# Modulation sums from GpSimd to VectorE, and column sums by transposes between feed-forward steps, in a two-part transformer kernel

## The reference

```
# first block, per layer (the mixer is "even" in layer 0, "odd" in layer 1)
h = h + 0.5 * rmsnorm(swiglu(rmsnorm(h, nw[0]), ...), nw[1])     # D_FF = 2816
h = h + rmsnorm(mixer(rmsnorm(h, nw[2])), nw[3])
h = h + 0.5 * rmsnorm(swiglu(rmsnorm(h, nw[4]), ...), nw[5])

# second block, per layer i
mod_l = silu(c) @ ada_w[i] + ada_b[i]          # (1024) @ (1024, 6144)
mod_c = silu(c_ctx) @ ada_w[i] + ada_b[i]      # only its first 2048 values, and only in layer 0, are used
sh1, sc1, g1, sh2, sc2, g2 = split(mod_l, 6)
h = rms_norm(x, norm1_g[i]) * (1 + sc1) + sh1
x = x + g1 * (diff_attention(h, h_c) if i == 0 else fourier_mix(h))
h2 = rms_norm(x, norm2_g[i]) * (1 + sc2) + sh2
x = x + g2 * (swiglu_2(h2) if i == 0 else moe_swiglu(h2))        # D_FF_2 = 3584, 8 experts
out = rms_norm(x, final_g)
```

## Time and profile before

| | |
|---|---|
| runs | 2940.45, 2946.97, 2948.32 us; median 2946.97 |
| profiled execution | span 2946.9 us from the first to the last instruction; its time is not given apart from the span |
| TensorE | 2758.8 us busy, 94%; mean granted clock 0.963 |
| VectorE | 2085.5 us busy, 71% |
| ScalarE | 1680.7 us busy, 57% |
| GpSimd | 590.6 us busy, 20% |
| DMA | 664.55 MB, mean 226 GB/s |
| chain that ended last | TensorE 81%, VectorE 12%, ScalarE 4%, issue 2% |

### The profile page before, as it was taken

The page is one execution under the profiler, slowest core; times in us unless marked ns, Lnnn a source line. Parts: engine busy times, 40 slices in busy tenths (PEclk is TensorE's granted clock), DMA queues, the critical chain, the costliest instruction groups (busy, mean ns, idle before and its releaser), DMA issues.

```text
span 2946.9 us, 35814 instructions
## 1 busy us (share of the span) xinstructions
PE 2758.8 (94%) x12921; PEld 2256.2 (77%) x12921; DVE 2085.5 (71%) x2339; ACT 1680.7 (57%) x2177; POOL 590.6 (20%) x321
## 2 busy tenths in 40 slices
PE   7999899989999999979669998799999999999997
PEld 6888778878987778868448886687878778787885
DVE  4556757678457755552557874699988989998897
ACT  4456454454367764432444442277787877778775
POOL 2000029999100000013009993000000000000000
PEclk9999999999899999989779999799999999999999
DMA  8555137678443345532028882299999999999994
GB/s 285 187 163 181 36 136 243 229 264 285 144 147 118 115 165 188 185 106 79 0 85 282 289 285 97 78 346 329 351 350 341 350 335 353 339 351 340 346 355 163
DMA packets 278012, 664.55 MB, mean 226 GB/s; under 512 B 12868, under 2 KB 21344, under 8 KB 277904
## 3 DMA queue, kind: packets, MB, share of 16 engines
q1 hardware_dynamic: 263344, 609.74, 58.4%
q0 software_dynamic: 14560, 53.36, 5.5%
HBM read 662.00 MB, written 1.05 MB: 225 GB/s over the span
## 4 chain that ended last, share of the span: by engine, by line
PE 81%; DVE 12%; ACT 4%; issue 2%; DMA 0%; DVEq 0%; ACTq 0%; SPq 0%
PE ps L2206 24%; PE ps L2208 24%; PE ps L2207 24%; DVE w_lo L1398 4%; ACT w_hi L742 2%; PE ps L2322 1%; PE ps L2388 1%; PE ps L2892 1%; PE ps L2806 1%; DVE xt L2078 1%; DVE small L1964 1%; PE ps L2768 1%; PE ps L2596 0%; DVE xn L1477 0%; PE ps L2850 0%
## 5 line engine op out<-in xcount | busy, mean ns | idle before, releaser
L1398 DVE TENSOR_TENSOR w_lo<-w_raw,w_hi 128x1024 fp32r<-128x1024 f32 x1156 | 1520.1, 1339 | 496.6 <-ACT w_hi L742 470.9
L742 ACT ACTIVATE w_hi<-w_raw 128x1024 fp32r<-128x1024 f32 x1156 | 1210.9, 1058 | 844.2 <-PE ps L2208 843.3
L2206 PE MATMUL ps<-w_hi,act_hi 128*128 128x512 f32 (+1 forms) x3424 | 1351.1, 395 | 50.7 <-DVE w_lo L1398 33.2
L2208 PE MATMUL ps<-w_lo,act_hi 128*128 128x512 f32 (+1 forms) x3424 | 1326.7, 387 | 0.0
L2207 PE MATMUL ps<-w_hi,act_lo 128*128 128x512 f32 (+1 forms) x3424 | 1325.6, 387 | 0.0
L2206 PEld LDWEIGHTS ps<-w_hi,act_hi 128*128 128x128 f32 x3424 | 650.2, 190 | 198.8 <-DVE w_lo L1398 53.9
L2208 PEld LDWEIGHTS ps<-w_lo,act_hi 128*128 128x128 f32 x3424 | 649.5, 190 | 132.6
L2207 PEld LDWEIGHTS ps<-w_hi,act_lo 128*128 128x128 f32 x3424 | 651.1, 190 | 126.0 <-issue 2.9
L621 POOL TENSOR_TENSOR scr<-scr 128x1024 f32<-128x1024 f32 x98 | 285.5, 2913 | 8.2
L619 POOL TENSOR_SCALAR scr<-scr,small 128x1024 f32<-128x1024 f32 x98 | 189.5, 1934 | 6.4
L602 POOL DMA_DIRECT2D scr<-in_ada_w x48 | 36.8, 766 | 401.7 <-DVE h L1482 382.3
(11 more groups left out here) (454 smaller groups left out, 1682.0 us busy)
## 6 DMA issues: line engine op xcount, KB each, us to landing
w_raw<-in_moe_w SPq DMA_DIRECT2D x336, 1024.0 KB, 6.8
scr<-in_ada_w POOLq DMA_DIRECT2D x48, 1024.0 KB, 5.9
w_raw<-in_ffn_w_gate SPq DMA_DIRECT2D x44, 1024.0 KB, 5.3
w_raw<-in_ffn_w_up SPq DMA_DIRECT2D x44, 1024.0 KB, 5.3
w_raw<-in_ffn_w_down SPq DMA_DIRECT2D x44, 1024.0 KB, 4.9
w_raw<-in_ff_w SPq DMA_DIRECT2D x42, 1024.0 KB, 5.7
w_raw<-in_odd_w_in SPq DMA_DIRECT2D x20, 1024.0 KB, 5.1
w_raw<-in_even_w_in SPq DMA_DIRECT2D x14, 1024.0 KB, 5.2
```

The source lines that it names most:

```text
L742: act.activation(w_hi[:, g % SPLITS, 0:c * width], w_raw[:, s % RING, o:o + c * width], ACT.Copy).then_inc(hi_done, 1)
L1398: dve.tensor_tensor(w_lo[:, g % SPLITS, 0:c * width], w_raw[:, s % RING, o:o + c * width], w_hi[:, g % SPLITS, 0:c * width].bitcast(F32), ...
L2206: pe.matmul(out_ap, hi, whi, start=start, stop=False)
L2208: return pe.matmul(out_ap, hi, wlo, start=False, stop=stop)
```

## The change

GpSimd keeps only the loads of the weight chunks, each released by a count of sums (`ada_sum`). The sums are done by VectorE as one instruction each, dst = w * x + dst (`accumulate`): 64 for layer 0, 48 for layer 1. They are strewn between the `w_lo` of the second and third feed-forward (layer 0, 0.625 for each granule) and of the dense one (layer 1, 0.6875 for each granule); a credit counter decides behind which.

The sum over partitions is now: TensorE transposes a block of 128x1024 sums in eight 128x128 transposes into banks 4 and 5 (`turn_sums`), once silu has read these; VectorE adds up each 128 columns of the result (`column_sums`) into `m_cols`. There are eight such windows for layer 0 (`SUMS_FIRST`, `SUMS_SECOND`: two in the second feed-forward, one in every step of the third) and six for layer 1 (`SUMS_DENSE`: steps 1 to 6). TensorE's gate matmuls of the next step wait for the adds (`mod_red`). The small instructions that make `modv` and `modc` follow once per layer.

```diff
 def modulation(l):          # GpSimd
     load(0)
     load(1)
     for j in range(24):
-        nb, k = divmod(j, 4)
-        cols = slice(DM * nb, DM * (nb + 1))
-        pool.wait_ge(ada_in[j % 2], n(ada_in[j % 2], 16))
-        for c in range(2):
-            sums = [(m_sumc, 8)] if l == 0 and nb < 2 else []
-            for dst, of in sums + [(m_sum, 0)]:
...
-                pool.tensor_scalar(product, w, x, 0.0, ALU.mult, ALU.add).then_inc(ada_mul, 1)
-                pool.wait_ge(ada_mul, n(ada_mul))
-                pool.tensor_tensor(dst[:, cols], dst[:, cols], product, ALU.add).then_inc(ada_sum, 1)
-            pool.wait_ge(ada_sum, n(ada_sum, 1 + len(sums)))
+        n(ada_sum, 4 if l == 0 and j < 8 else 2)
         if j + 2 < 24:
+            pool.wait_ge(ada_sum, n.last(ada_sum))
             load(j + 2)

+SUMS_FIRST = {3: 0, 4: 6}
+SUMS_SECOND = {0: 1, 1: 7, 2: 2, 3: 3, 4: 4, 5: 5}
+SUMS_DENSE = {i + 1: i for i in range(6)}
+SUM_RATE = (0.625, 0.6875)

+def accumulate(l, i):       # VectorE
+    if l == 0 and i < 32:
+        j, c, context = i // 4, i % 4 // 2, i % 2
+    else:
+        j, c, context = (i - 16 * (l == 0)) // 2, i % 2, 0
+    nb, k = divmod(j, 4)
+    dst = (m_sumc if context else m_sum)[:, DM * nb:DM * (nb + 1)]
+    of = 8 * context + 2 * k + c
+    w, x = m_w[:, j % 2, c, :], silc[:, of:of + 1]
+    if c == 0 and not context:
+        dve.wait_ge(ada_in[j % 2], n(ada_in[j % 2], 16))
+    if k == 0 and c == 0:
+        dve.tensor_scalar(dst, w, x, None, ALU.mult).then_inc(ada_sum, 1)
+    else:
+        dve.wait_ge(ada_sum, n.last(ada_sum))
+        dve.scalar_tensor_tensor(dst, w, x, dst, ALU.mult, ALU.add).then_inc(ada_sum, 1)
+    n(ada_sum)

 def lo(k):                  # VectorE, behind each w_lo
+    if layer[0] is not None and at_sum[0] < (48 if layer[0] else 64):
+        credit[0] += SUM_RATE[layer[0]]
+        if credit[0] >= 1:
+            credit[0] -= 1
+            accumulate(layer[0], at_sum[0])
+            at_sum[0] += 1

 def gated(...):             # VectorE, step i; layer[0] = sums from behind step 0's first lo to the loop's end
     dve... hp               # the product of step i
+    if windows and i in windows:
+        column_sums(windows[i])
     if i:
         lo(1)

+def column_sums(nb):        # VectorE
+    dve.wait_ge(mod_tp, n(mod_tp))
+    for q in range(2):
+        ins = dve.tensor_reduce(m_cols[:, 8 * nb + 4 * q:8 * nb + 4 * q + 4],
+                                ps[:, 4 + q, :].rearrange("p (c n) -> p c n", c=4), AX_X, ALU.add)
+    ins.then_inc(mod_red, 1)
+    n(mod_red)

-def mod_columns(l, half):   # VectorE; called twice for each layer
+def mod_columns(l):         # once: behind the third feed-forward; before the dense feed-forward's add_branch
...

 def gated(...):             # TensorE, step i
     pe.wait_ge(silu_done, n(silu_done))
+    if windows and i - 1 in windows:
+        pe.wait_ge(mod_red, n(mod_red))
     up(...)                 # gate
     up(...)                 # up
+    if windows and i in windows:
+        turn_sums(sums, windows[i])
     down(...)               # of step i - 1
     hidden(i)

-def mod_columns(l, half):   # TensorE
-    for k in range(24 * half, 24 * half + 24):
-        ins = pe.matmul(ps[:, 4 + half, k:k + 1], m_sum[:, k * P:(k + 1) * P], ones[:, 0:1], start=True, stop=True)
...
+def turn_sums(l, nb):       # TensorE
+    context = nb >= 6
+    ready = 16 * (nb % 6) + 16 if l == 0 and nb % 6 < 2 else 8 * nb + 16 * (1 - l) + 8
+    pe.wait_ge(ada_sum, 64 * l + ready)
+    pe.wait_ge(silu_done, n.last(silu_done) + 1)
+    src = m_sumc[:, DM * (nb - 6):DM * (nb - 5)] if context else m_sum[:, DM * nb:DM * (nb + 1)]
+    for q in range(8):
+        ins = pe.transpose(ps[:, 4 + q // 4, (q % 4) * P:(q % 4 + 1) * P], src[:, q * P:(q + 1) * P], ident)
+    ins.then_inc(mod_tp, 1)

-tail(gated(FF1, scaled=True), 0)
+tail(gated(FF1, scaled=True, sums=0, windows=SUMS_FIRST), 0)
-tail(gated(FF1, scaled=True, closing=columns), 4)
+tail(gated(FF1, scaled=True, sums=0, windows=SUMS_SECOND), 4)
-gated(FF2)
+gated(FF2, sums=1, windows=SUMS_DENSE)
-mod_columns(1, 0)           # behind row_broadcast; and mod_columns(1, 1) at the head of experts
```

More of the change, by code:

```diff
@@ L1513, in start, with gated @@
                 next_rstd()
-            def gated(ff, tbs=TB, beside=None, scaled=False):
+            def gated(ff, tbs=TB, beside=None, scaled=False, sums=None, windows=None):
                 s = steps(ff)
@@ L1529, in gated @@
                         lo(per)
+                    layer[0] = sums
                     if i:
@@ L1551, in gated @@
                         beside(i)
+                layer[0] = None
                 hidden(len(s) - 1)
@@ L1919, in odd @@
                     ins.then_inc(og_lo, 1)
-            def mod_columns(l, half):
-                dve.wait_ge(mod_col, n(mod_col))
-                at_col, v = 24 * half, V_ADAB + 48 * l + 24 * half
-                link(dve.tensor_tensor(modv[:, at_col:at_col + 24], ps[:, 4 + half, at_col:at_col + 24], colv[:, v:v + 24], ALU.add))
-                a, g = modv[:, at_col + 8:at_col + 16], (V_N2 if half else V_N1) + 8 * l
-                link(dve.scalar_tensor_tensor(a, a, 1.0, colv[:, g:g + 8], ALU.add, ALU.mult))
-                if l == 0 and half == 0:
-                    link(dve.tensor_tensor(modc, ps[:, 4, 48:64], colv[:, V_ADAB:V_ADAB + 16], ALU.add))
+            def mod_columns(l):
+                v = V_ADAB + 48 * l
+                dve.wait_ge(mod_red, n.last(mod_red))
+                if l:
+                    dve.wait_ge(diag_done, 2)
+                link(dve.tensor_tensor(modv[:, 0:48], m_cols[:, 0:48], colv[:, v:v + 48], ALU.add))
+                if l == 0:
+                    dve.tensor_tensor(modc, m_cols[:, 48:64], colv[:, V_ADAB:V_ADAB + 16], ALU.add)
+                for at_col, g in ((MOD_A1, V_N1), (MOD_A2, V_N2)):
+                    a = modv[:, at_col:at_col + 8]
+                    ins = dve.scalar_tensor_tensor(a, a, 1.0, colv[:, g + 8 * l:g + 8 * l + 8], ALU.add, ALU.mult)
+                link(ins)
+                if l == 0:
                     a = modc[:, MOD_A1:MOD_A1 + 8]
@@ L2170, in _ @@
             boundary(1.0, nw(0, 4), 0)
-            gated(FF1, scaled=True)
+            gated(FF1, scaled=True, sums=0, windows=SUMS_FIRST)
             boundary(0.5, nw(1, 0), 0)
-            gated(FF1, scaled=True)
-            mod_columns(0, 0)
-            mod_columns(0, 1)
+            gated(FF1, scaled=True, sums=0, windows=SUMS_SECOND)
+            mod_columns(0)
+            at_sum[0], credit[0] = 0, 0
             boundary(0.5, nw(1, 2), 4)
@@ L2309, in norm, with gated @@
                     pe.wait_ge(alo_done, n.last(alo_done))
-            def gated(ff, tbs=TB, beside=None, scaled=False, closing=None):
+            def gated(ff, tbs=TB, beside=None, scaled=False, closing=None, sums=None, windows=None):
                 s = steps(ff)
@@ L2344, in gated @@
                 n(silu_done)
+                if windows and last in windows:
+                    n(mod_red)
                 early = 1 if tbs == TB else 2
@@ L2759, in odd @@
                 return [o_slot(c) for c in range(12, 16)], [(og_lo, 7), (og_lo, 8)]
-            def mod_columns(l, half):
-                context = l == 0 and half == 0
-                for nb in range(3 * half, 3 * half + 3):
-                    n(ada_sum, 16 if context and nb < 2 else 8)
-                pe.wait_ge(ada_sum, n.last(ada_sum))
-                for k in range(24 * half, 24 * half + 24):
-                    ins = pe.matmul(ps[:, 4 + half, k:k + 1], m_sum[:, k * P:(k + 1) * P], ones[:, 0:1], start=True, stop=True)
-                if context:
-                    for k in range(16):
-                        ins = pe.matmul(ps[:, 4, 48 + k:49 + k], m_sumc[:, k * P:(k + 1) * P], ones[:, 0:1], start=True, stop=True)
-                ins.then_inc(mod_col, 1)
+            def turn_sums(l, nb):
[7 more added lines that the diff above has]
+                ins.then_inc(mod_tp, 1)
             def diff_attention():
@@ L2863, in experts @@
             def experts():
-                mod_columns(1, 1)
                 pe.wait_ge(diag_done, n(diag_done))
@@ L2937, in more_rows @@
                 pe.transpose(ps[:, 4, 256:384], scr[:, 3 * P:4 * P], ident).then_inc(more_t, 1)
-            def columns():
-                mod_columns(0, 0)
-                mod_columns(0, 1)
             pe.wait_ge(rows_c, 1)
@@ L2963, in _ @@
             norm(lead=True)
-            gated(FF2)
+            gated(FF2, sums=1, windows=SUMS_DENSE)
             row_broadcast()
-            mod_columns(1, 0)
             fourier()
```

15 lines of the change are left out of this document (7 added, 8 removed).

## The result

| | before | after |
|---|---|---|
| median (lowest to highest) | 2947.64 us (2940.45 to 2951.71), 4 runs | 2923.03 us (2920.29 to 2927.81), 4 runs |
| profiled execution's span | 2946.9 us | 2926.0 us (its own time 2927.81) |

The ratio is 0.992, 95% interval 0.9905 to 0.9935: 0.8% faster. Forecast: 2924 us, range 2914 to 2938. The same program in a second set of runs gave 2924.12 us (0.992, 0.99 to 0.994). The profiled execution is the longest of its four, so its span fell by less (20.9 us) than the median (24.6 us).

What follows compares the result with a forecast made beforehand. TensorE's own stream was taken to bound the feed-forwards, VectorE's speed the stretches between stages. Gains of 35.7 us less 11.4 and 1.35 left 22.9, from 2946.9 to 2924 us; range 2914 to 2938.

Steps and rivals of the forecast that it cites:

- Column sums of layer 0: Behind the feed-forward with columns, removing the one-column matmuls and the low clock after them gains 25.7 us.
- Boundary at 600: From first xn to the next feed-forward's first hidden transpose, VectorE without GpSimd's sums beside it gains 5.25 us.
- Behind the dense feed-forward: VectorE's wbc to w_lo chain without GpSimd gains 2.35 us, old column work removed 0.4; together 2.75 us.
- Contention inside the three feed-forwards: First to last hidden transpose without GpSimd working: 1.2 us gained in two feed-forwards, 0.8 in the dense one.
- 13 windows: Eight added transposes each in TensorE's stream inside the feed-forwards cost 0.88 us a window, 11.4 us in all.
- The first rival: Dear windows: each window of transposes costs 1.7 us, 10.7 us more in all, 2935 us; chance 0.09.
- Window at step 0: Where no down work covers it, VectorE's two sums from PSUM delay the w_lo that TensorE needs: 1.35 us lost.
- Sums on VectorE: The 64 and 48 sums, 1.16 us each, fit VectorE's room in the feed-forwards and cost zero.
- Column adds and loads: Column adds on VectorE ahead of the boundary and add_branch, and loads on GpSimd's queue, cost zero.
- The second rival: VectorE becomes the bound in the feed-forwards if a sum takes 2.3 us: 2927 to 2966 us; chance 0.06.
- The third rival: Late modulation weight chunks make VectorE wait, with w_lo behind: 66 us, 2990 us, slower; chance 0.05.
- The fourth: Windows let TensorE's clock fall, 2.6 us each, 36 us in all: 2960 us, slower; chance 0.04.

Runs made afterwards that it cites:

- e3: The changed kernel with every window's eight transposes done twice into the same banks; 2936.95 us, ratio 0.9965 to the kernel before.
- e8: The changed kernel with the window at step 0 of the third feed-forward moved to step 5 of the second; 2929.70 us, ratio 0.994.
- e2: The changed kernel with sums on VectorE, but the old one-column matmuls at their old places and no windows; 2942.54 us, ratio 0.9987.
- e9: The changed kernel with GpSimd given 152 rounds of unrelated elementwise work, paced to bring back only the contention; 2954.23 us, ratio 1.0028.
- e4: The changed kernel with every multiply-add on VectorE followed by a second one with factor 0; 2938.42 us, ratio 0.9971.
- e6: The changed kernel with layer 1's first 24 one-column matmuls put back, results unused, in TensorE's pause before the Fourier mix; 2925.00 us, ratio 0.9927.
- e10: The changed kernel with unused 128x512 matmuls in three TensorE pauses, behind attention, the dense feed-forward and the Fourier mix; 2917.50 us, ratio 0.9907.
- e5: The changed kernel with GpSimd given 266 rounds of unrelated elementwise work ahead of the loads, which made chunks late; 3109.26 us, ratio 1.055.
- e11: The changed kernel with four more transposes, 0.4 us, in the last window of the third feed-forward; 2926.67 us, ratio 0.9936.

## Why the prediction was right

The span fell by 20.9 us, from 2946.9 to 2926.0, where 22.9 were forecast. Term by term, as gain, forecast against measured:

- **Column sums of layer 0**: 25.7; measured 35.9 - 10.3 = 25.6.
- **Boundary at 600**: 5.25; measured 5.4. In six later profiles it is 31.7 to 31.8 us long (the further 1.4 is the clock step), in e3 and e8 33.3 and 33.4. The forecast put the whole term down to VectorE's slower instructions. That is so for the waiting (TensorE's idle time fell by 3.85 us in e2); the rest came with the clock, and e9, which slowed VectorE again, brought back waiting but no low clock.
- **Behind the dense feed-forward**: 2.75; measured 12.9 - 10.1 = 2.8 from wbc to xn, and 3.0 came back in e9.
- **Contention inside the three feed-forwards**: 1.2 + 0.8 = 2.0; measured by e2, which has no windows: 152.5 - 150.1, less the clock step of 1.7, which the kernel before has there and e2 has not, so 0.7, then 0.6 and 0.6: 1.9.
- **13 windows**: -11.4, 0.88 each. Measured 199.8 - 194.3 = 5.5 for the dense feed-forward's six (0.92 each), 154.6 (e8) - 150.0 (the fourth feed-forward, clean and without the step) = 4.6 for five, 151.9 - 150.0 = 1.9 for two: 12.0. e3 gives 0.8 to 0.94 for one more. The first rival (1.7 us a window) falls. Its price was also read wrong: it took one record of a one-column matmul for the whole matmul, which has two.
- **Window at step 0**: -1.35; measured 1.2, in the timeline and by e8.
- **Sums on VectorE**: 0. The sums' row shows 1.28 us, but that is a duration, and the forecast's 1.16 was counted from start to start; so counted a sum takes 1.19 (1604.74 to the w_lo at 1605.93). The duration is 0.06 longer than that of the same instruction with a constant factor (1.28 and 1.22 in e4). Nothing hung on it: TensorE's waits for w_lo over the whole span are 31.6 us (33.2 before), and e4 puts the edge somewhere below twice the load.
- **Column adds and loads**: 0. The adds of layer 1 stand ahead of the 8.62 us in which VectorE idles, no instruction waited for a load, and the third feed-forward's tail to xn shows no more than the first's (10.3 and 10.6 us).

Measured terms: 25.6 + 5.4 + 2.8 + 1.9 - 12.0 - 1.2 = 22.5 us. The 1.6 us that the span lacks are the balance of stages that the change does not edit and of the clock. Gained: the step at the head of three feed-forwards, some 4.8, and 0.5 at the start; 1.6 of the 4.8, at the fourth feed-forward, come and go between kernels that don't edit it. Lost: 3.5 in the Fourier stretch, 1.9 in attention, 1.1 in the experts, 0.3 in the odd mixer. These sum to -1.5.

So the large terms were right one by one, but that the span came so close is in part luck: movements of the clock, none of them in the working, cancelled. One is the step, which I took for a part of a feed-forward's length. Another is the Fourier stretch. I wrote that the one-column matmuls of layer 1 run while TensorE waits anyway and that "removing them gives nothing by itself". TensorE's pause grew from 8.86 to 11.67 us, and the matmuls behind it ran at the low clock for longer. That the removed matmuls were the cause is not shown, and e6 speaks against it: it puts back all 24 that stood in this pause and stays at 61.7. That a filled pause is the remedy is not shown for this stretch either, since e3 and e4 have 60.0 us there with the pause empty. It is shown for the pause behind the Fourier mix (e10: 1.8 us).

**The second rival** rested on the rule of the Trainium skill (Vector Engine (DVE) Microarchitecture Reference, "Points that are easy to get wrong") of half throughput for a scalar_tensor_tensor with two non-bf16 SBUF sources. The trace does not agree: this very form, both sources f32 in SBUF, took 1279 ns for 1024 columns, 1.25 ns a column, against 1222 ns for w_lo. The rival's threshold of 2.2 us was not tested; 1.28 us a sum cost nothing and 2.5 us cost 15 us (e4). **The third rival** is a real chain (e5) which the delays here don't reach. **The fourth** did not come by the windows: the granted clock is 1.00 with 48 window transposes in the dense feed-forward.

**What stays open.** The odd mixer took 233.1 to 233.6 us in eight of the profiles, and 235.8, 237.3 and 238.8 in e3, e2 and e8. The profiles show that the difference is TensorE at the low clock for longer, with the same idle time. Why the clock falls there for longer in these three was not found. It isn't the one-column matmuls ahead of it, which the kernel before has as well (233.1 us), and e11 says that a shift of 0.4 us isn't enough. It is worth up to 5.5 us, as much as a term of the sum.
